# Two block-triangular inverses with products on crossed quadrants, predicated copies for the corrections, and later correction products

## Chip, cores and metric

One NeuronCore of a Trainium2 chip runs the whole kernel in one launch. The metric is the device time of an execution in microseconds, the median of several.

## What is computed

Six layers on 256 tokens of width 1024, float32 in and out: layers 0 and 3 are gated DeltaNet layers ("gdn"), layer 1 is HGRN2, layer 2 is GLA, layers 4 and 5 mix four heads' kinds. Each has a projection, a mixer, an output projection and a SwiGLU feed-forward. The change touches the gdn mixer. Its core, cut from the reference:

```python
L = jnp.where(strict, jnp.einsum('bhncd,bhnsd->bhncs', kb, k) * decay, 0.0)
rhs = jnp.concatenate([v * beta[..., None], kb * jnp.exp(G)[..., None]], axis=-1)
sol = lax.linalg.triangular_solve(L + jnp.eye(CHUNK), rhs, left_side=True, lower=True)
```

The kernel works with chunks of 128 tokens, so it needs (I + L)^-1 for 16 matrices of 128x128: 8 heads times 2 chunks, numbered j.

## The kernel before

**The inverse.** A 128x128 inverse is made of its two diagonal 64x64 blocks, which sit on partitions 0 to 63 and 64 to 127, and one off-diagonal block. The 64x64 blocks grow by doubling: at level lv, blocks of size 2^lv are joined to blocks of twice the size. X is the inverse so far, XT its transpose, and C the part of L that this level joins; the correction is X C X. The 16 matrices go in four groups of four (`GROUPS = (0, 2, 1, 3)`), one PSUM bank a group. For levels 1 to 5 a group takes these steps:

- POOL multiplies `lb` (the 64x64 blocks of L) by the mask of the level into `lb_masked` (L1571), once a level and group.
- PE: the product `cx` of `lb_masked` with X, 8 matmuls of 64x64x64 (L981). A float32 matmul is two records in a profile, each with a weight load.
- ACT copies the product from PSUM to `cx` (tile yb).
- PE: the two corrections, for X and XT, 16 matmuls into the two halves of one bank (`gdn_correct`, L1055).
- DVE subtracts the bank from X and XT in one operation of 128x512 (`corrected`).

PE's order is product of group n, then correction of group n-1. Level 6 makes the off-diagonal block with four plus four single matmuls a group (L984, L1050). Then come the products with the values (L994 on). All matmuls of levels 1 to 5 use the array's two diagonal quadrants: rows 0 to 63 to columns 0 to 63, and rows 64 to 127 to columns 64 to 127.

**What sets the order.** Each engine's program is written out by hand, and semaphores tie them: a `tick` with a key raises one, `wait_ge(*sig.at(key))` waits for it. The eight PSUM banks are claimed by PE in turn (`psum.claim`): a claim of a bank waits until the reader of its last use has released it. In a gdn layer the last projection units have other work between them on PE: `gdn_values` (transposes of v), `gdn_columns` (four small transposes, bank "tok") and two `gdn_spread`. DVE runs beside it `setup` (layer 0), `decay_rows`, `unit_qk` (eight multiplications, each behind an ACT pair), `gdn_columns` (copies the bank "tok") and `gdn_values`. Then the loop over eight heads makes scores, `lt` and `at`, and the inverse begins.

Of the kernel before, what the change touches and what calls it, by code (L numbers as in the profile page):

```python
# [24 lines left out]
U32 = mybir.dt.uint32  # L25
# [192 lines left out]
def build(nc, A, out, book, layers=len(CHAIN)):  # L218

    book.restart()  # L220
    with ExitStack() as ctx:
# [46 lines left out]
        level = sb("level", [P, 7, P])  # L268
        level64 = sb("level64", [P, 6, HALF2])
        ident64 = sb("ident64", [P, HALF2])  # L270
# [75 lines left out]
        blocks = (slice(0, HALF2), slice(HALF2, HALF))  # L346
        xx = flat(inv[:, 0:16, :]).rearrange("p (g two j n) -> p g two j n", g=4, two=2, j=4)
# [7 lines left out]
        def transposed(j):  # L355
            return xx[:, j // 4, 1, j % 4, :]
# [18 lines left out]
        def halves(ap, lv, which):  # L375


            return ap.rearrange("p h (n two c) -> p h n two c", two=2, c=1 << lv)[:, :, :, which, :]

# [142 lines left out]
        def _(pe):  # L522
# [128 lines left out]
            def project(layer, kind, norm):  # L651
                nonlocal unit
                psum.next = 4
                for n, (c0, w, how, name, idx) in enumerate(units_in(kind)):
# [38 lines left out]
                    if kind == "gdn" and n >= N_CONV + 1:  # L693
                        qk_sums(layer, ((0, 1, 2), (3, 4, 5), (6, 7), ())[n - N_CONV - 1])
                    if kind == "gdn" and n == N_CONV + 3:
# [209 lines left out]

            def normed_rows(n):
# [48 lines left out]
            def gdn(layer):  # L955
# [11 lines left out]
                for lv in range(1, 7):  # L967
                    for n, g in enumerate(GROUPS):
                        if lv == 1 and n == 2:
                            gdn_transpose(layer, g)  # L970
                            gdn_correct(layer, lv, GROUPS[1])
                            gdn_transpose(layer, GROUPS[3])
                        b = psum.claim(pe, "cx", layer, lv, g)
                        if lv < 6:
                            pe.wait_ge(*pool_gdn.at("masked", layer, lv, g))
                        pe.wait_ge(*(act_gdn.at("X", layer, g) if lv == 1 else dve_gdn.at("X", layer, lv - 1, g)))
                        for j in range(4 * g, 4 * g + 4):
                            cols_of = slice((j % 4) * HALF2, (j % 4 + 1) * HALF2)
                            if lv < 6:
                                for r in blocks:  # L980
                                    m = nc.tensor.matmul(b[r, cols_of], lb_masked[r, j, :], inverse(j)[r, :], start=True, stop=True)  # L981
                            else:
                                t0 = (j // 8) * T
                                m = nc.tensor.matmul(b[HALF2:HALF, cols_of], lt[0:HALF2, j % 8, t0 + HALF2:t0 + HALF], inverse(j)[0:HALF2, :],  # L984
                                                     start=True, stop=True)
                        m.then_inc(*pe_gdn.tick("cx", layer, lv, g))
                        if n and (lv, n) != (1, 2):
                            gdn_correct(layer, lv, GROUPS[n - 1])
                    gdn_correct(layer, lv, GROUPS[3])
# [40 lines left out]
            def gdn_transpose(layer, g):  # L1030
# [3 lines left out]
                for j in range(4 * g, 4 * g + 4):  # L1034
                    for r in blocks:
                        m = nc.tensor.matmul(b[r, (j % 4) * HALF2:(j % 4 + 1) * HALF2], transposed(j)[r, :], ident[r, r],
                                             start=True, stop=True)
                m.then_inc(*pe_gdn.tick("transposed", layer, g))

            def gdn_correct(layer, lv, g):  # L1040


                b = psum.claim(pe, "z", layer, lv, g)
                pe.wait_ge(*act_gdn.at("cx", layer, lv, g))
                if lv == 6:
                    pe.wait_ge(*dve_gdn.at("XT", layer, 5, g))
                for j in range(4 * g, 4 * g + 4):
                    c = (j % 4) * HALF2
                    if lv == 6:
                        m = nc.tensor.matmul(b[0:HALF2, c:c + HALF2], cx[HALF2:HALF, j, :], inv[HALF2:HALF, 16 + j, HALF2:HALF],  # L1050
                                             start=True, stop=True)
                        continue
                    for left, right, c in ((transposed(j), cx[:, j, :], c), (cx[:, j, :], transposed(j), c + T)):
                        for r in blocks:
                            m = nc.tensor.matmul(b[r, c:c + HALF2], left[r, :], right[r, :], start=True, stop=True)  # L1055
# [423 lines left out]
        def _(pool):  # L1479
# [45 lines left out]
            for lv in range(7):  # L1525
                h = 1 << lv
                m = level[:, lv, :].rearrange("p (n a c) -> p n a c", a=2, c=h)
# [29 lines left out]
            for layer, (kind, _) in enumerate(CHAIN[:layers]):  # L1557
# [8 lines left out]
                early, late = GROUPS[:2], GROUPS[2:]  # L1566
                steps = [(lv, q) for of in (early, late) for lv in range(2) for q in of]
                for lv, q in steps + [(lv, q) for lv in range(2, 6) for q in GROUPS]:
                    pool.wait_ge(*(act_gdn.at("blocks", layer, q) if lv == 0 else
                                   dve_gdn.at("XT", layer, 0, q) if lv == 1 else pe_gdn.at("cx", layer, lv - 1, q)))  # L1570
                    g.tensor_tensor(lb_masked[:, 4 * q:4 * q + 4, :], lb[:, 4 * q:4 * q + 4, :],  # L1571
                                    level64[:, lv:lv + 1, :].to_broadcast([P, 4, HALF2]), ALU.mult)\
# [1426 lines left out]
```

## Time and profile before

| | |
|---|---|
| median of 3 runs | 2128.95 us (2126.13 to 2129.04) |
| profiled execution | 2127.26 us, its span 2125.6 us |
| PE busy | 2071.8 us, 97% of the span |
| DVE, ACT, POOL busy | 1498.4, 891.4, 177.8 us |
| the chain that ended last | PE 84%, DVE 9%, ACT 3%, issue 2% |

A profile lists when each instruction of each engine ran. "Releaser" is the instruction whose semaphore ended a wait; "issue" is idle time in which the engine waited for nothing that the profile shows. PEclk 1.00 is TensorE at 2.4 GHz, 0.50 at 1.2 GHz.

### The profile page before, as it was taken

Reading aid. Unit: us, or ns where it says so; the run is one execution under the profiler, and the core shown is the slowest. Engines: PE = TensorE matmul, PEld = TensorE weight load, DVE = VectorE, ACT = ScalarE, POOL = GpSimd, SP = SyncE. Lnnn points to the kernel's source line nnn. Section 1 sums busy time; section 2 is a strip of 40 time slices with the busy share of each in tenths; the row PEclk is TensorE's granted clock in tenths of the full one; section 3 lists DMA queues with packets and bytes.
Section 4 is the critical chain, followed back from the end, with each engine's and each line's share of the span. In section 5 each row is a group of like instructions: output and inputs, shape, how many; then the busy total and the mean of one; then the engine's idle time right before and its main releaser. Section 6 shows DMA issues by size and latency. Waiting matters only on the chain.

```text
span 2125.6 us, 35623 instructions
## 1 busy us (share of the span) xinstructions
PE 2071.8 (97%) x14377; PEld 1801.8 (85%) x14377; DVE 1498.4 (70%) x1949; ACT 891.4 (42%) x1174; POOL 177.8 (8%) x152
## 2 busy tenths in 40 slices
PE   8999999999999999999899999998989999999999
PEld 8988888798888798888798978887869998778998
DVE  6968754778745677654697684456688887588887
ACT  3244444334444423444323444445564334664332
POOL 6630000000000000000073300000100000100000
PEclk9999999999999999999999999999999999999999
DMA  8512665552655553655464046654325555414552
GB/s 249 178 42 80 201 195 181 176 185 95 198 181 194 161 179 121 203 192 181 147 188 140 3 161 205 193 181 157 101 77 182 178 190 165 138 50 162 196 178 99
DMA packets 267625, 333.81 MB, mean 157 GB/s; under 512 B 20562, under 2 KB 230613, under 8 KB 267493
## 3 DMA queue, kind: packets, MB, share of 16 engines
q1 hardware_dynamic: 267493, 331.93, 48.2%
q8 instruction: 98, 1.61, 0.3%
q14 instruction: 34, 0.28, 0.0%
HBM read 330.84 MB, written 1.05 MB: 156 GB/s over the span
## 4 chain that ended last, share of the span: by engine, by line
PE 84%; DVE 9%; ACT 3%; issue 2%; SPq 1%; DMA 0%; POOL 0%; DVEq 0%; ACTq 0%
PE bank L586 47%; PE bank L554 26%; DVE pj L2187 2%; PE bank L1055 2%; ACT stat L1578 1%; PE bank L819 1%; PE bank L911 1%; PE bank L981 1%; PE bank L637 1%; PE bank L1136 1%; DVE w_hi L2226 1%; DVE sq L2187 1%; DVE pj L2181 1%; DVE w_lo L2228 1%; DVE xt L2187 1%
## 5 line engine op out<-in xcount | busy, mean ns | idle before, releaser
L2228 DVE TENSOR_TENSOR w_lo<-ring,w_hi 128x2048 fp32r<-128x2048 f32 (+2 forms) x289 | 615.2, 2131 | 373.7 <-ACT w_hi L1623 371.3
L1623 ACT ACTIVATE w_hi<-ring 128x2048 fp32r<-128x2048 f32 (+1 forms) x220 | 418.9, 1905 | 474.8 <-PE bank L586 287.3
L586 PE MATMUL bank<-w_lo,xh 128*128 128x512 f32 x992 | 267.3, 392 | 0.0
L586 PE MATMUL bank<-w_hi,xl 128*128 128x512 f32 x896 | 240.6, 390 | 1.0 <-DVE xl L2177 1.0
L586 PE MATMUL bank<-w_hi,xh 128*128 128x512 f32 x896 | 240.9, 391 | 0.6 <-ACT xh L1578 0.6
L554 PE MATMUL bank<-xh,w_hi 128*128 128x256 f32 x1752 | 240.0, 290 | 1.6 <-DVE pj L2177 0.8
L554 PE MATMUL bank<-xh,w_lo 128*128 128x256 f32 (+2 forms) x1832 | 241.4, 284 | 0.0
L554 PEld LDWEIGHTS bank<-xh,w_hi 128*128 128x128 f32 x1752 | 225.0, 195 | 11.4 <-issue 6.7
L554 PEld LDWEIGHTS bank<-xh,w_lo 128*128 128x128 f32 (+2 forms) x1832 | 228.8, 191 | 0.8
L554 PE MATMUL bank<-xl,w_hi 128*128 128x256 f32 x1752 | 229.3, 283 | 0.0
L554 PEld LDWEIGHTS bank<-xl,w_hi 128*128 128x128 f32 x1752 | 218.5, 192 | 0.4
L586 PEld LDWEIGHTS bank<-w_lo,xh 128*128 128x128 f32 x992 | 184.8, 188 | 38.0 <-DVE w_lo L2228 0.7
L586 PEld LDWEIGHTS bank<-w_hi,xh 128*128 128x128 f32 x896 | 167.1, 188 | 37.5 <-issue 2.0
L586 PEld LDWEIGHTS bank<-w_hi,xl 128*128 128x128 f32 x896 | 167.5, 188 | 36.8 <-DVE xl L2177 2.3
L1545 POOL TENSOR_TENSOR w_lo<-ring,w_hi 128x1536 fp32r<-128x1536 f32 x26 | 104.5, 4017 | 950.3 <-DVE w_hi L2226 950.3
L586 PE MATMUL bank<-w_hi,hid_hi 128*128 128x512 f32 x528 | 167.3, 398 | 2.0 <-DVE hid_lo L2177 2.0
L586 PE MATMUL bank<-w_hi,hid_lo 128*128 128x512 f32 x528 | 163.4, 390 | 0.0
L586 PE MATMUL bank<-w_lo,hid_hi 128*128 128x512 f32 x528 | 163.0, 390 | 0.0
L1578 ACT ACTIVATE yb<-bank 128x256 f32<-128x256 f32 (+4 forms) x146 | 58.9, 403 | 165.2 <-PE bank L586 124.9
L586 PEld LDWEIGHTS bank<-w_hi,hid_lo 128*128 128x128 f32 x528 | 99.1, 188 | 21.5
L586 PEld LDWEIGHTS bank<-w_lo,hid_hi 128*128 128x128 f32 x528 | 99.1, 188 | 21.4
L586 PEld LDWEIGHTS bank<-w_hi,hid_hi 128*128 128x128 f32 x528 | 94.6, 189 | 19.5 <-DVE hid_lo L2177 3.7
(325 smaller groups left out, 2409.2 us busy)
## 6 DMA issues: line engine op xcount, KB each, us to landing
ring<-in_ffn_w_in_dram SPq DMA_DIRECT2D x264, 512.0 KB, 4.4
ring<-in_ffn_w_down_dram SPq DMA_DIRECT2D x88, 512.0 KB, 4.2
ring<-in_gdn_w_in_dram SPq DMA_DIRECT2D x64, 512.0 KB, 5.0
ring<-in_ffn_w_out_dram SPq DMA_DIRECT2D x44, 512.0 KB, 3.9
ring<-in_w_in_dram SPq DMA_DIRECT2D x40, 512.0 KB, 4.8
ring<-in_hgrn_w_in_dram SPq DMA_DIRECT2D x32, 512.0 KB, 4.6
ring<-in_gla_w_in_dram SPq DMA_DIRECT2D x24, 512.0 KB, 4.7
ring<-in_gdn_w_out_dram SPq DMA_DIRECT2D x16, 512.0 KB, 4.5
```

Of the source, the lines that this page charges most:

```text
L554: m = nc.tensor.matmul(cols, *((wk, xk) if tokens == ALL else (xk, wk)), start=(first and step == 0 and k == 0 and (j % 2 == 0)), stop=(la ...
L586: m = nc.tensor.matmul(bank[:, 0:width], xin[:, k0 + k, rows_of], w[:, k, c * width:(c + 1) * width], start=(first and step == 0 and k == ...
L637: m = nc.tensor.transpose(b[:, j * P:(j + 1) * P], src[:, t, c * CHUNK + j * P:c * CHUNK + (j + 1) * P], ident[:, :])
L819: m = nc.tensor.transpose(banks[6][:, j * T + t * HALF:j * T + (t + 1) * HALF], hidt[:, t, j * P:(j + 1) * P], ident[:, :])
L911: nc.tensor.matmul(b[:, 0:T], k[:, 0:HALF], q[:, :], start=True, stop=True)
L981: m = nc.tensor.matmul(b[r, cols_of], lb_masked[r, j, :], inverse(j)[r, :], start=True, stop=True)
L1055: m = nc.tensor.matmul(b[r, c:c + HALF2], left[r, :], right[r, :], start=True, stop=True)
L1545: g.tensor_tensor(w_lo[:, unit % RING, part], ring[:, unit % RING, part], high_part(unit)[:, part], ALU.subtract).then_inc(*pool_lo.tick())
L1578: nc.scalar.activation(out_, in_, func, **kw).then_inc(*sig.tick(*key))
L1623: nc.scalar.activation(taken(high_part(u), u), taken(ring[:, u % RING, :], u), ACT.Copy).then_inc(*act_hi.tick())
L2187: v.scalar_tensor_tensor(out=out_, in0=a, scalar=s1, in1=b, op0=op0, op1=op1).then_inc(*sig.tick(*key))
L2228: v.tensor_tensor(w_lo[:, u % RING, 0:share], w[:, 0:share], high[:, 0:share], ALU.subtract).then_inc(*dve_lo.tick())
```

## The change

- `lb` is now copied with factor -1, so that it holds -L. Levels 1 to 4 use it whole, without a mask; POOL's masks remain for level 5 alone (4 operations in place of 24 a layer), and POOL fills XT with the identity ahead of the stage.
- XT is kept on the other half of the partitions than before, so products and the correction of X go from rows r to the other half's columns (`crossed`), while the correction of XT goes from rows r to columns r. The two corrections go to two banks, "z" and "zt".
- What a whole-block product puts outside the blocks of the level is left out when DVE puts the correction in by `copy_predicated`, under the level's mask for XT and its transpose for X, two operations of 128x128 elements a group, and four of 64x128 in place of two subtractions where the stage starts.
- PE's order is product of group n, then correction of group n-2.
- At level 5 the correction of X for the second half is left out (12 matmuls for 16).
- The transposed masks are made once, in layer 0: four PE transposes behind `qk_sums` of unit N_CONV + 2, and two DVE copies ahead of `gdn_columns` in unit N_CONV + 4. The tile `level` keeps four levels; two more are built in `dec`.

The core of the diff (the first `masks_transposed` is PE's, the second DVE's):

```diff
+            def masks_transposed():
+                b = psum.claim(pe, "level masks")
+                pe.wait_ge(*pool_setup.at("constants"))
+                for lv in range(1, 5):
+                    m = nc.tensor.transpose(b[:, (lv - 1) * P:lv * P], level_mask(lv), ident[:, :])
+                m.then_inc(*pe_setup.tick("level masks"))
...
+                gdn_product(layer, 1, GROUPS[0])
+                gdn_product(layer, 1, GROUPS[1])
+                gdn_correct(layer, 1, GROUPS[0])
+                gdn_transpose(layer, GROUPS[2])
+                gdn_correct(layer, 1, GROUPS[1])
+                gdn_transpose(layer, GROUPS[3])
+                gdn_product(layer, 1, GROUPS[2])
+                gdn_product(layer, 1, GROUPS[3])
+                for lv in range(2, 7):
                     for n, g in enumerate(GROUPS):
...
+                        gdn_product(layer, lv, g)
+                        gdn_correct(layer, lv if n > 1 else lv - 1, GROUPS[n - 2])
+                gdn_correct(layer, 6, GROUPS[2])
+                gdn_correct(layer, 6, GROUPS[3])
...
-                    for left, right, c in ((transposed(j), cx[:, j, :], c), (cx[:, j, :], transposed(j), c + T)):
-                        for r in blocks:
-                            m = nc.tensor.matmul(b[r, c:c + HALF2], left[r, :], right[r, :], start=True, stop=True)
+                    for r, to in crossed:
+                        if lv < 5 or to == blocks[0]:
+                            nc.tensor.matmul(b[to, of], transposed(j)[r, :], cx[r, j, :], start=True, stop=True)
+                        m = nc.tensor.matmul(bt[r, of], cx[r, j, :], transposed(j)[r, :], start=True, stop=True)
...
+            def masks_transposed():
+                dve.wait_ge(*pe_setup.at("level masks"))
+                masks = psum.bank("level masks")[:, :].rearrange("p (l n) -> p l n", l=4)
+                for r in blocks:
+                    v.tensor_copy(level64_t[r, :, :], masks[r, :, r]).then_inc(*dve_setup.tick("level masks"))
+                psum.release(dve_setup, "level masks")
...
+                    if layer == 0 and n == N_CONV + 4:
+                        masks_transposed()
                     if kind == "gdn" and n == N_CONV + 4:
                         gdn_columns(layer)
...
-                        X = xx[:, g, :, :, :].rearrange("p two j n -> p (two j n)")
-                        tt(s, X, X, b[:, :], ALU.subtract, "X", layer, lv, g)
+                        put(("X", lv, g), xx[:, g, 0, :, :], 0, level64_t[:, lv - 1:lv, :], by_head(b))
+                        put(("XT", lv, g), xx[:, g, 1, :, :], 1, level64[:, lv:lv + 1, :], by_head(bt))
```

PE's queue in layer 0, from the sums of squares to the next projection unit. Each row is a kind of matmul with the semaphores that it waits for. Before (L943 are the transposes of v, L933 those of "tok", L951 `gdn_spread`, L554 the projection):

```order
L925 MATMUL bank<-yb,ones 128x512 [waits act_gdn] x2
L943 MATMUL bank<-ident,pj 128x128 [waits act_proj,act_gdn]
L943 MATMUL bank<-ident,pj 128x128 x3
...
L933 MATMUL bank<-ident,rows 128x8 [waits dve_gdn,act_gdn,dve_setup]
L933 MATMUL bank<-ident,rows 128x8 x3
```

Of the change, the same place (L959, L949 and L967 are the same steps):

```order
L941 MATMUL bank<-yb,ones 128x512 [waits act_gdn] x2
L959 MATMUL bank<-ident,pj 128x128 [waits act_proj]
L959 MATMUL bank<-ident,pj 128x128 x3
...
L949 MATMUL bank<-ident,rows 128x8 [waits dve_gdn,dve_setup]
L949 MATMUL bank<-ident,rows 128x8 x3
```

The four mask transposes stand one unit ahead and took a bank more, so the banks have moved on by one. The claim of the bank for "tok" waited for an ACT release (act_gdn); now it waits for the release of the bank "level masks", which is the twelfth tick of dve_setup (the wait for dve_setup that stood there before was for its first tick).

DVE's queue at the same place. Before:

```order
L2638 CAST rows_hi<-rows 8x512 [waits act_gdn,dve_gdn]
L2177 TENSOR_TENSOR rows_lo<-rows,rows_hi 8x512 [waits dve_gdn]
L2177 TENSOR_TENSOR pj<-pj,stat 128x512 [waits act_gdn] x8
L2646 COPY cols<-bank 128x4x8 [waits pe_gdn]
L2177 TENSOR_TENSOR vb<-bank,cols 128x512 [waits pe_gdn,dve_gdn]
```

Of the change:

```order
L2678 CAST rows_hi<-rows 8x512 [waits act_gdn,dve_gdn]
L2207 TENSOR_TENSOR rows_lo<-rows,rows_hi 8x512 [waits dve_gdn]
L2207 TENSOR_TENSOR pj<-pj,stat 128x512 [waits act_gdn] x8
L2286 COPY level_t<-bank 64x256 [waits pe_setup]
L2286 COPY level_t<-bank 64x256
L2686 COPY cols<-bank 128x4x8 [waits pe_gdn]
L2207 TENSOR_TENSOR vb<-bank,cols 128x512 [waits pe_gdn,dve_gdn]
```

The two copies that release the bank stand behind all eight multiplications of `unit_qk`.

PE's queue in the middle of the inverse, product and the first matrix's corrections. Before, and of the change behind it:

```order
L981 MATMUL bank<-inv,ct 64x64 x8
L1055 MATMUL bank<-yb,inv 64x64 x2
L1055 MATMUL bank<-inv,yb 64x64 x2
L1055 MATMUL bank<-yb,inv 64x64 x2
L1055 MATMUL bank<-inv,yb 64x64 x2
```

```order
L1063 MATMUL bank<-inv,ct 64x64 x8
L1083 MATMUL bank<-yb,inv 64x64
L1084 MATMUL bank<-inv,yb 64x64
L1083 MATMUL bank<-yb,inv 64x64
L1084 MATMUL bank<-inv,yb 64x64
```

The count of matmuls of a group and level is the same, 24; the corrections alternate between the two banks and touch all four quadrants within four matmuls.

## Rows read from the trace of the kernel before

**Rows 1.** The page: busy time of engines, and the last chain by engine

```profile
PE 2071.8 (97%) x14377; PEld 1801.8 (85%) x14377; DVE 1498.4 (70%) x1949; ACT 891.4 (42%) x1174; POOL 177.8 (8%) x152
PE 84%; DVE 9%; ACT 3%; issue 2%; SPq 1%; DMA 0%; POOL 0%; DVEq 0%; ACTq 0%
```

**Rows 2.** Windows over both inverses: length, busy and instructions by engine, clock, DMA

```profile
133.73:173.07 39.34, 37.47 (x1097) 35.71 (x1097) 21.62 (x40) 15.96 (x38) 14.96 (x21) 1.00 0.01 4
1176.01:1214.44 38.43, 37.12 (x1098) 35.53 (x1097) 21.61 (x40) 15.96 (x38) 14.95 (x21) 1.00 0.02 4
```

**Rows 3.** Timeline, PE, level 3: start, length, line, operation, count of records

```profile
147.35 0.63 PE L981 MATMUL bank<-inv,ct 64*64 64x64 f32 x16
147.82 0.28 PE L1055 MATMUL bank<-yb,inv 64*64 64x64 f32 x4
...
148.75 0.63 PE L981 MATMUL bank<-inv,ct 64*64 64x64 f32 x16
```

**Rows 4.** Windows, PE alone, between stalls: length, busy (matmul records), clock, DMA

```profile
146.02:149.65 3.63, 3.63 (x125) 1.00 0.02 5
161.43:165.62 4.19, 4.09 (x127) 1.00 0.01 4
165.62:169.51 3.89, 3.83 (x127) 1.00 0.02 4
```

**Rows 5.** DMA of 146 to 170 us: GB/s in 40 slices, and by queue

```profile
GB/s 0 0 27 0 0 0 0 0 27 0 0 0 0 27 0 0 0 0 0 0 0 27 0 0 0 0 0 0 27 0 0 0 0 0 27 0 0 0 0 0
...
q8 instruction: 6, 0.10, 1.5%
```

**Rows 6.** Timeline, PE, at two breaks in the stream (idle before, releaser)

```profile
146.02 0.39 PE L981 MATMUL bank<-inv,ct 64*64 64x64 f32 x7 [0.67 <-issue]
...
1203.50 0.31 PE L1055 MATMUL bank<-yb,inv 64*64 64x64 f32 x4
1203.85 0.33 PE L1055 MATMUL bank<-inv,yb 64*64 64x64 f32 x4
```

**Rows 7.** Timeline, PE, where level 5 meets level 6 (L984: rows 0-63 to columns 64-127)

```profile
169.06 0.22 PE L1055 MATMUL bank<-inv,yb 64*64 64x64 f32 x1
169.11 0.22 PE L984 MATMUL bank<-inv,mats 64*64 64x64 f32 x1
169.11 0.22 PE L1055 MATMUL bank<-inv,yb 64*64 64x64 f32 x2
169.17 0.22 PE L984 MATMUL bank<-inv,mats 64*64 64x64 f32 x1
```

**Rows 8.** Timeline, PE, end of level 6 and the first product behind it

```profile
171.92 1.22 PE L1050 MATMUL bank<-inv,yb 64*64 64x64 f32 x16
173.07 2.05 PE L994 MATMUL bank<-vb,inv 128*128 128x128 f32 x16
```

**Rows 9.** Timelines, PE and DVE, layer 0 ahead of the scores; a pair of 64x256 bank reads

```profile
112.01 0.41 PE L933 MATMUL bank<-ident,rows 8*128 8x8 f32 x4
...
113.55 0.38 PE L554 MATMUL bank<-xh,w_hi 128*128 128x256 f32 x1
...
114.20 0.69 DVE L2177 TENSOR_TENSOR pj<-pj,stat 128x512 f32<-128x512 f32 x1 [0.55 <-ACT stat L1578]
114.81 0.18 DVE L2646 COPY cols<-bank 128x32 f32<-128x32 f32 x1
...
1212.60 0.91 DVE L2181 TENSOR_SCALAR inv<-bank 64x256 f32<-64x256 f32 x2
```

**Rows 10.** Timeline, PE, at a long wait, and the window behind it (clock second from the end)

```profile
1053.70 0.66 PE L637 MATMUL bank<-ident,xt 128*128 128x128 f32 x2 [3.86 <-DVE xt L2187]
1050.20:1057.10 6.90, 3.04 (x13) 2.28 (x13) 6.59 (x12) 3.65 (x6) 0.00 (x0) 0.51 0.26 82
```

**Rows 11.** DVE's predicated copies of 128x256, levels 0 and 1, then 2 and 3 (ns)

```profile
L2838 DVE COPY_PREDICATED mats<-level,bank x8: 739/774/807, 491.4 to 499.4; 128x256 f32<-128x256 uint32 x8
...
L2838 DVE COPY_PREDICATED mats<-level,bank x8: 424/429/441, 501.3 to 508.0; 128x256 f32<-128x256 uint32 x8
```

More of the change, by code:

```diff
@@ L346, in build @@
         blocks = (slice(0, HALF2), slice(HALF2, HALF))
+        crossed = ((blocks[0], blocks[1]), (blocks[1], blocks[0]))
         xx = flat(inv[:, 0:16, :]).rearrange("p (g two j n) -> p g two j n", g=4, two=2, j=4)
@@ L378, in halves, with level_mask @@
             return ap.rearrange("p h (n two c) -> p h n two c", two=2, c=1 << lv)[:, :, :, which, :]
+        def level_mask(lv):
+            return level[:, lv, :] if lv < WHOLE_BLOCKS else dec[:, lv - WHOLE_BLOCKS, 0:P]
         def par(col):
@@ L694, in project @@
                         qk_sums(layer, ((0, 1, 2), (3, 4, 5), (6, 7), ())[n - N_CONV - 1])
+                    if layer == 0 and n == N_CONV + 2:
+                        masks_transposed()
                     if kind == "gdn" and n == N_CONV + 3:
@@ L1034, in gdn_transpose, with gdn_product @@
                 for j in range(4 * g, 4 * g + 4):
-                    for r in blocks:
-                        m = nc.tensor.matmul(b[r, (j % 4) * HALF2:(j % 4 + 1) * HALF2], transposed(j)[r, :], ident[r, r],
+                    for r, to in crossed:
+                        m = nc.tensor.matmul(b[to, (j % 4) * HALF2:(j % 4 + 1) * HALF2], transposed(j)[r, :], ident[r, r],
                                              start=True, stop=True)
                 m.then_inc(*pe_gdn.tick("transposed", layer, g))
+            def gdn_product(layer, lv, g):
+                b = psum.claim(pe, "cx", layer, lv, g)
+                pe.wait_ge(*(act_gdn.at("X", layer, g) if lv == 1 else dve_gdn.at("X", layer, lv - 1, g)))
+                if lv == 1:
+                    pe.wait_ge(*act_gdn.at("blocks", layer, g))
+                if lv == 5:
+                    pe.wait_ge(*pool_gdn.at("masked", layer, g))
+                for j in range(4 * g, 4 * g + 4):
+                    of = slice((j % 4) * HALF2, (j % 4 + 1) * HALF2)
+                    if lv == 6:
+                        t0 = (j // 8) * T
+                        m = nc.tensor.matmul(b[HALF2:HALF, of], lt[0:HALF2, j % 8, t0 + HALF2:t0 + HALF], inverse(j)[0:HALF2, :],
+                                             start=True, stop=True)
+                        continue
+                    for r, to in crossed:
+                        m = nc.tensor.matmul(b[to, of], (lb_masked if lv == 5 else lb)[r, j, :], inverse(j)[r, :], start=True, stop=True)
+                m.then_inc(*pe_gdn.tick("cx", layer, lv, g))
@@ L1524, in _ @@
             keep(rot96[:, 80:96], [[-1, 16]], -64, 1, op=ALU.not_equal, fill_=1.0)
[L1525 removed]
+            for lv in range(6):
                 h = 1 << lv
[L1527 removed]
+                m = level_mask(lv).rearrange("p (n a c) -> p n a c", a=2, c=h)
                 fill(m[:, :, 0, :], 0.0)
@@ L1565, in _ @@
                 g.memset(inv[:, 16:32, 0:HALF2], 0.0).then_inc(*pool_gdn.tick("cleared", layer))
[L1566 to L1570, printed above, removed]
+                for q in GROUPS:
+                    g.tensor_copy(xx[:, q, 1, :, :], ident64[:, :].rearrange("p (a n) -> p a n", a=1).to_broadcast([P, 4, HALF2]))\
+                        .then_inc(*pool_gdn.tick("identity", layer, q))
+                for q in GROUPS:
+                    pool.wait_ge(*act_gdn.at("blocks", layer, q))
                     g.tensor_tensor(lb_masked[:, 4 * q:4 * q + 4, :], lb[:, 4 * q:4 * q + 4, :],
-                                    level64[:, lv:lv + 1, :].to_broadcast([P, 4, HALF2]), ALU.mult)\
-                        .then_inc(*pool_gdn.tick("masked", layer, lv, q))
+                                    level64[:, 5:6, :].to_broadcast([P, 4, HALF2]), ALU.mult)\
+                        .then_inc(*pool_gdn.tick("masked", layer, q))
         @block.scalar
@@ L1961, in diagonal_blocks @@
                     for r in blocks:
-                        run(s, lb[r, 4 * g:4 * g + 4, :], lt[r, h0:h0 + 4, t0 + r.start:t0 + r.stop], ACT.Copy, "blocks", layer, g)
+                        run(s, lb[r, 4 * g:4 * g + 4, :], lt[r, h0:h0 + 4, t0 + r.start:t0 + r.stop], ACT.Copy, "blocks", layer, g,
+                            scale=-1.0)
                 for h in range(8):
```

75 lines of the change are left out of this document (35 added, 40 removed).

## The prediction

> **What bounds the kernel now.** I read the page first: PE is busy for 97% of the span and carries 84% of the chain that ended last [rows 1]. So the change is worth what it takes from, or adds to, PE's own sequence. Then the windows over the two inverses: 39.34 and 38.43 us, PE busy for all but 1.9 and 1.3 us of them, DVE for 21.6, ACT 16.0, POOL 15.0 [rows 2]. Nothing but PE can be the bound there, and the most that is at stake is some 78 us.
>
> What is PE's pace in there? From product to product one group takes 148.75 - 147.35 = 1.40 us for 48 records, of which the 16 of the product take 0.47 [rows 3]: 29.2 ns a record, with two quadrants at work, so about 58 ns a record in one quadrant. Read alone, this says that four quadrants would halve the corrections. Before I believe it I ask what else could set 29 ns.
>
> The stream breaks where nothing is waited for: 0.67 us of "issue" at 146.02, and at 1203.50 four records take 0.35 us where others take 0.12 [rows 6]. Between such breaks lie 125 to 127 matmul records, each with its weight load: 256 instructions, within the few records that a trace misses. It takes 3.63, 4.19 and 3.89 us to go through them [rows 4]. In the same stretch the only DMA traffic is the queue that brings instructions: 6 packets, 0.10 MB, so 16 KB each, which are 256 instructions of 64 bytes, and they come 5 to 8 slices of 0.6 us apart, 3.0 to 4.8 us [rows 5]. So a packet is asked for when a block is begun, and PE stands at a block's end if the next one has not come. At 29.2 ns, 128 records take 3.74 us; a packet's round takes 3.6 to 4.2. The stream of instructions and the array are level now, and from 146.02 to 169.51 six blocks took 3.92 us each. I take the fetch as the bound of the stage.
>
> The Trainium skill speaks against this: "Runtime: NRT & Kernel Launch", section "Instruction fetch mechanics", says that the sequencer streams pages of 256 instructions while it runs the current one, that a boundary's cost is mostly hidden, and gives PE a store of 2048 instructions. The trace has the pages of 256, but not the hiding: the breaks at 146.02 and 1203.50. By that page the stage would go at the array's pace, which is the third rival below.
>
> **The change part by part.**
>
> *Levels 1 to 5.* A group and level keeps 24 matmuls, 96 instructions, and its waits. At a fixed round a block, four levels of quicker array buy nothing: 3.9 us for 256 instructions before and after. I take 3.9, the mean of the three lengths; bounds 3.5, between the near packets of rows 5, and 4.2. The start of the stage (transposes, ACT's blocks of `lb`) keeps its ACT and PE steps; the one packet that ends late (the break at 146.02) is in the same place. Nothing there.
>
> *Fewer instructions.* Level 5 drops 4 matmuls in each of four groups, 64 instructions; the second claim of a bank and the split waits add about 16. That is 48 fewer of some 2,200, and they are missed at the end, after the last block has arrived, where level 6 goes one quadrant at a time: 16 records took 1.22 us [rows 8]. 24 records at 58 ns are 1.4 us. In layer 0 the masks' transposes shift the blocks by 10 instructions and leave 1.1. Sum over both layers: -2.5 us, bounds 0 and -4.
>
> *DVE.* One 128x512 subtraction of 0.69 us makes way for two predicated copies of 128 elements. The trace has them with 256 elements: 0.77 us at levels 0 and 1 and 0.43 at 2 and 3 [rows 11]. Half the elements cannot cost more, so a pair is at most 1.54 and 0.86, and likelier 0.9 and 0.6. A group has 1.4 us of PE time, and DVE is busy for 21.6 of 39 us [rows 2]: hidden. If this cover were gone, a pair that is 0.2 us too slow for its group would cost 0.2 x 4 a level. *POOL* loses 20 masks a layer; PE had no wait for them past the first level. Nothing. *Corrections two groups behind* give ACT's copy a longer time; PE's waits in the stage are under 2 us with the breaks [rows 2], and in a stream held by fetches such a wait was already under the fetch. Nothing.
>
> *The masks' transposes, and the bank that they hold.* This is the dear part, and it is in layer 0 alone. The transposes of 128x128 cost PE 4 x 0.11 us. Their bank is released by two DVE copies that stand behind the eight multiplications of `unit_qk`, and the turn of the banks gives just this bank to "tok". PE does "tok" at 112.01 and the next projection unit at 113.55; DVE ends the eighth multiplication at 114.81 [rows 9]. The copies read 64x256 from a bank; two such reads took 0.91 us [rows 9]. `setup` has two small copies more, 0.1 us. So the release comes at 114.81 + 0.1 + 0.9, and "tok" starts at 115.9, which is 3.9 us late. From there PE needs 1.3 us of work to the projection unit, of which 0.25 was a wait: it starts at 117.2 for 113.55. **+3.6 us**, the transposes' 0.44 hidden in it. Queued behind the wait on PE are "tok", two spreads, the projection unit and then the scores, and PE has no wait afterwards in which this could drown. Bounds: +3.0 if the copies take 0.3 each, +4.0.
>
> *The clock.* In that wait PE stands for about 3.4 us, from 112.5 to 115.9. The trace has a wait of 3.86 us that ends at 1053.7; over 6.9 us around it the granted clock was 0.51, and of these PE had work in about 3.4, which then took twice its time [rows 10]. [...] I take +1.3; bounds 0 and 3.4.
>
> **Sum.** +3.6 + 1.3 - 2.5 = +2.4 us. The profiled execution of 2127.26 us (span 2125.6 and 1.7 around it) would take 2129.7. The median of the runs shown lies 1.7 above the profiled one, so I forecast **2131.3 us**. 0.2% is 4.3 us, about what a measurement of this kernel can tell from no change: no change that can be told.
>
> **The rivals.**
>
> *Quicker rounds (15%).* If a packet is asked for earlier once PE drains a block faster, a round may be 3.5 us, as the nearest packets stand [rows 5]. Seven rounds a layer at 0.4 less: -5.6 us, 2125.7. Against it: the rounds that began behind a break were 3.63 to 4.19 [rows 4].
>
> *The wait is not there (8%).* If "tok" came before or ACT's chain freed DVE earlier, +3.6 and +1.3 fall away: 2126.4. Against it stands the order of the two queues.
>
> *Four quadrants pay (8%).* If the breaks are not what bounds the stream, a quadrant's own pace does. A crossed quadrant then has 16 records of 58 ns a group, 0.93 us for 1.40: -0.47 x 20 groups a layer, and the breaks' 1.0 go too, so -10.4 a layer and 2131.3 - 20.8 + 2.5 = 2113. That quadrants do overlap is shown: around 169.1 L984 in a third quadrant runs beside L1055 in two, 5 records within 0.11 us [rows 7]. This is what the Trainium skill, "TensorEngine Tiling (Array Packing)", section "Key Properties", promises for 64x64 tiles, and here the trace agrees for three. The page "TensorE: Matmul & The Clock Gate" (section "Wait — 56ns, not 53.3ns?") puts a floor of 25 ns between starts; by it the corrections would take 0.80 for 0.93 us a group and the gain would be a quarter of this. The change may also fail to overlap at all, if matmuls start in order; under the fetch that gives the forecast's time too.
>
> *The wait costs the clock for longer (17%).* This one ends slower. If the clock falls for 6.9 us as in rows 10 and all of it meets projection work, the price is 3.4 for 1.3: 2133.4. It decides from 3.2 us on.
>
> **How the numbers follow.** Forecast 52%, within 2127.5 to 2134.5; the rivals 15, 8, 8 and 17%. 8 in 10 reaches to the quick rounds with the full saving at the end below, and to the long clock with rounds of 4.1 above (14 x 0.2 = 2.8): 2122 to 2136. Faster by over 0.2% (under 2124.7): the four quadrants, half of the quick rounds and a little of the rest, 20%. Slower by over 0.2% (over 2133.2): half of the long clock and a sixth to a third of the forecast's case, 25%. Within: 55%.
>
> **What would show it.** In the changed kernel's trace: the windows of both inverses 37 to 38.5 us; breaks every 128 matmul records, now at nearly every block, with idle "issue" in place of busy time and PE's busy share in the stage well down; six to seven instruction packets in 24 us as before; records within a block closer than 29 ns. In layer 0 an idle PE of 3 to 4 us ahead of the "tok" transposes with DVE as its releaser, and perhaps a granted clock of 0.5 behind it; none in layer 3. It is wrong if packets come every 2.5 us, if the stage is under 33 us, or if "tok" does not wait.

## The result and the profile after

| | time | against the kernel before |
|---|---|---|
| the kernel before, in the same runs | 2126.51 us (median of 17) | |
| the changed kernel | 2132.1 us (median of 17, 2129.81 to 2139.32) | 1.0028, interval 1.0021 to 1.0034 |
| its profiled execution | span 2129.3 us | +3.7 over the span of 2125.6 |

The change costs 5.6 us, by the interval 4.5 to 7.2, so it is a change that can be told. The forecast of 2131.3 us lies 0.8 below the median, but part of that closeness is luck: I added +2.4 us to a median of 3 runs, 2128.95, which stands 2.4 above the median of 17. The effect itself is more than twice the 2.4 us that I forecast.

The page of the changed kernel, the lines that answer to [rows 1]:

```profile
PE 2055.0 (97%) x14317; PEld 1784.9 (84%) x14317; DVE 1500.1 (70%) x1995; ACT 890.9 (42%) x1174; POOL 151.3 (7%) x116
...
PE 82%; DVE 11%; issue 3%; ACT 3%; SPq 1%; DMA 0%; DVEq 0%; ACTq 0%
```

PE has 16.8 us less busy time and the kernel is longer: what the array saved became waiting. The windows of both inverses, to be held against [rows 2]:

```profile
137.40:176.49 39.09, 28.95 (x1066) 26.68 (x1065) 21.97 (x62) 15.91 (x38) 1.45 (x2) 1.00 0.01 3
1179.41:1218.88 39.47, 28.58 (x1066) 26.57 (x1065) 21.88 (x62) 15.79 (x38) 1.45 (x2) 1.00 0.02 4
```

PE is busy for 29 of 39 us, where it was for 37.5, and the length has not changed: -0.25 us in layer 0, +1.04 in layer 3. PE's timeline there (start, length, records, idle before and its releaser), one group and then the breaks, from several windows:

```profile
151.45 0.57 PE L1063 MATMUL bank<-inv,ct 64*64 64x64 f32 x13
...
152.38 0.51 PE L1063 MATMUL bank<-inv,ct 64*64 64x64 f32 x11
154.17 0.34 PE L1063 MATMUL bank<-inv,ct 64*64 64x64 f32 x5 [1.27 <-issue]
...
158.11 0.21 PE L1084 MATMUL bank<-inv,yb 64*64 64x64 f32 x1 [1.27 <-issue]
...
162.00 0.27 PE L1084 MATMUL bank<-inv,yb 64*64 64x64 f32 x1 [1.10 <-issue]
```

A group of 48 records takes 152.38 - 151.45 = 0.93 us, where it took 1.40 [rows 3]. Four quadrants do overlap: the 32 records of the corrections take some 0.46 us, 14.5 ns each. Then PE stands for 1.1 to 1.3 us with no releaser. The windows from break to break, as [rows 4] (PE alone; then three of layer 3 with all engines), and the DMA of 150 to 174 us, as [rows 5]:

```profile
150.23:154.17 3.94, 2.67 (x125) 1.00 0.02 4
154.17:158.11 3.94, 2.67 (x124) 1.00 0.02 4
158.11:162.00 3.89, 2.79 (x124) 1.00 0.02 4
...
1193.03:1197.26 4.23, 2.56 (x126) 2.42 (x125) 1.49 (x6) 1.29 (x3) 0.00 (x0) 1.00 0.02 4
1197.26:1201.57 4.31, 2.66 (x124) 2.52 (x124) 1.00 (x4) 2.30 (x5) 0.00 (x0) 1.00 0.02 4
1205.68:1209.34 3.66, 2.69 (x125) 2.59 (x125) 1.59 (x5) 1.15 (x3) 0.00 (x0) 1.00 0.02 4
```

```profile
GB/s 0 0 27 0 0 0 0 0 0 27 0 0 0 0 0 27 0 0 0 0 0 0 27 0 0 0 0 0 27 0 0 0 0 0 0 27 0 0 0 0
...
q8 instruction: 6, 0.10, 1.7%
```

124 to 126 records from one break to the next, 3.9 us in layer 0 and 3.7 to 4.3 in layer 3, six packets of instructions in 24 us, as before. The array needs 2.7 of each 3.9 us.

The other place is layer 0 ahead of the scores, [rows 9] before. PE's timeline, then DVE's:

```profile
104.12 2.18 PE L561 MATMUL bank<-xh,w_hi 128*128 128x256 f32 x16 [0.86 <-ACT stat L1607]
...
111.70 1.91 PE L959 MATMUL bank<-ident,pj 128*128 128x128 f32 x16
115.87 0.38 PE L949 MATMUL bank<-ident,rows 8*128 8x8 f32 x4 [2.26 <-DVE level_t L2286]
...
117.21 2.18 PE L561 MATMUL bank<-xh,w_hi 128*128 128x256 f32 x16
```

```profile
114.90 0.87 DVE L2286 COPY level_t<-bank 64x256 f32<-64x256 f32 x2
```

"tok" starts at 115.87 and the projection unit at 117.21, 3.66 us later than at 113.55, with DVE's mask copies as the releaser. Both profiles are level up to here (99.77 and 99.73 at the last projection records ahead of the sums of squares). From here every step stands 3.4 to 3.7 us later, up to the end of layer 0's inverse (176.49 for 173.07) and the start of layer 3's (1179.41 for 1176.01).

### The profile page after: what moved, and what is told of

It reads as the page before. It is cut to its first block, busy times and chain, and to the rows that moved or that the text cites. A ratio compares the mean times of both kernels' runs of the same rounds, so it can differ in the third digit from the quotient of the medians.

```text
span 2129.3 us, 35554 instructions
## 1 busy us (share of the span) xinstructions
PE 2055.0 (97%) x14317; PEld 1784.9 (84%) x14317; DVE 1500.1 (70%) x1995; ACT 890.9 (42%) x1174; POOL 151.3 (7%) x116
## 4 chain that ended last, share of the span: by engine, by line
PE 82%; DVE 11%; issue 3%; ACT 3%; SPq 1%; DMA 0%; DVEq 0%; ACTq 0%
PE bank L593 47%; PE bank L561 26%; DVE pj L2217 2%; ACT stat L1607 1%; PE bank L828 1%; PE bank L1165 1%; PE bank L644 1%; PE bank L1063 1%; DVE w_hi L2256 1%; DVE sq L2217 1%; DVE pj L2211 1%; PE bank L1084 1%; DVE mats L2207 1%; DVE w_lo L2258 1%; DVE sq L2207 1%
```

## The experiments

Each was timed beside the kernel before on the same chip. The ratio to that kernel is the number to compare; 0.001 is 2.1 us. The medians are of 11 executions, of 9 in e3 and of 5 in e9. The changed kernel and the twelve runs:

| | median us | ratio to before | interval |
|---|---|---|---|
| changed kernel | 2132.10 | 1.0028 | 1.0021 to 1.0034 |
| e1 POOL builds the masks | 2126.52 | 1.0008 | 0.9999 to 1.0017 |
| e2 two quadrants | 2130.39 | 1.0018 | 1.0009 to 1.0027 |
| e3 products as 128x128x64 | 2137.56 | 1.0070 | 1.0044 to 1.0097 |
| e4 copies early | 2126.18 | 1.0003 | 0.9994 to 1.0011 |
| e5 PE kept busy in the wait | 2129.09 | 1.0020 | 1.0011 to 1.0029 |
| e6 two quadrants, copies early | 2125.94 | 1.0002 | 0.9993 to 1.0011 |
| e7 e6, one first copy a group | 2125.08 | 0.9998 | 0.9989 to 1.0007 |
| e8 e6, one group behind | 2129.18 | 1.0018 | 1.0009 to 1.0028 |
| e9 e4 with padding matmuls | 2133.57 | 1.0034 | 1.0021 to 1.0048 |
| e10 before, two groups behind | 2124.84 | 0.9989 | 0.9980 to 0.9998 |
| e11 e7, POOL builds the masks | 2125.16 | 0.9990 | 0.9981 to 0.9999 |
| e12 e10, level 5 halved | 2124.43 | 0.9989 | 0.9980 to 0.9998 |

My theory: the inverse goes by the fetch of instructions, so quadrants bring nothing, and the masks' bank costs the time. The rivals: the stage itself got slower; the array's pace counts; the clock.

### The masks' bank: e1, e4

e1: POOL writes the transposed masks with its own patterns in its idle time of layer 0; PE's transposes, their bank and DVE's copies are gone.

```diff
-                    if layer == 0 and n == N_CONV + 2:
-                        masks_transposed()
...
+                        keep(both[r, :, 0, :], [[-2 * h, n], [0, h]], -h, 1)
+                        keep(both[r, :, 0, :], [[2 * h, n], [0, h]], 2 * h - 1, -1)
```

> The changed kernel, but POOL builds the transposed masks in its idle time of layer 0, so that PE's four mask transposes, their bank and DVE's two copies are gone; the rest is unchanged. Theory A (the masks' bank costs the time): the tok transposes stand near 112.0 again in place of 115.9 and the next projection unit near 113.6 in place of 117.2, the time falls by 3.6 us against the changed kernel (2132.1 to about 2128.5), and what is left over the kernel before is +1 to +2. Rival B (the inverse stage itself is slower, the wait is absorbed somewhere): the unit starts earlier but the time stays within 1 us of 2132.1. Rival C (the clock fell in the wait and costs besides): more than 4.5 us come back.

e4: in DVE's program only.

```diff
+                    if layer == 0 and n == N_CONV + 3:
+                        masks_transposed()
                     if kind == "gdn" and n > N_CONV:
                         unit_qk(...)
-                    if layer == 0 and n == N_CONV + 4:
-                        masks_transposed()
```

> The changed kernel with DVE's two copies of the transposed masks one unit earlier, ahead of the multiplications of unit_qk, so that the bank is free long before tok; PE's transposes and the turn of the banks stay. Theory A: the 2.3 us wait ahead of tok goes, but the bank that the masks took still makes the projection unit at 104.1 wait for ACT (0.86 us) behind 0.5 us of transposes, so that tok starts near 113.5 and 2 us of the 3.6 come back: about 2130. Rival B: all 3.6 come back, 2128.5. Rival C: the copies delay DVE's multiplications and with them the release that follows, and nothing comes back.

Both give back some 5 us (5.6 and 5.9 by medians, 4.3 and 5.3 by ratios), more than the 3.6 and 2 expected. The inverse's four quadrants are in both, so the bank is the cause. PE's timeline of e4 at the place:

```profile
111.75 1.91 PE L959 MATMUL bank<-ident,pj 128*128 128x128 f32 x16
113.59 0.41 PE L949 MATMUL bank<-ident,rows 8*128 8x8 f32 x4
...
114.95 1.22 PE L561 MATMUL bank<-xh,w_hi 128*128 128x256 f32 x8
```

The wait is gone; the unit starts 2.26 us earlier. It is still 1.4 later than before, by the transposes and the 0.86 us wait at 104.12, which I had not seen: the claim moved the turn of the banks, and the unit now waits for an ACT release. In e1 the unit that waited at 104.12 starts at 101.99, and the later one so:

```profile
113.73 2.17 PE L561 MATMUL bank<-xh,w_hi 128*128 128x256 f32 x16 [0.51 <-ACT stat L1613]
```

That is 1.2 us earlier than in e4, yet e1 is no faster; 1.2 us lies within both intervals, so this isn't resolved. Such places can be compared only between profiles that are level ahead of them: in those of e6, e10 and e11 PE is 1.5 us later already at 84 us, with the same program up to there. And 2.26 us of lateness does not explain 5: what else goes with the wait is in e5.

### The clock behind the wait: e5

```diff
                         gdn_values(layer)
+                        if layer == 0:
+                            stay_awake(5, (psum.next + 1) % 8)
```

> The changed kernel with five matmuls of 128x256 (0.4 us each, their result unused) ahead of the tok transposes in layer 0, into the bank of the spread that follows, so that PE has work in the 2.3 us in which it waits for the release of the masks' bank. In two of three profiles of kernels with this wait the granted clock fell to 0.50 right behind it and the projection unit took 3 us longer. Theory A (the wait's price is 3.6 us of lateness and, in many executions, up to 3 us of halved clock): tok still starts near 115.9, the clock stays at 1.00 behind it, and the median falls by 1 to 2.5 us against the changed kernel's 2132.1. Rival B (the clock has no part in the median): no change, or +0.2 from the fillers' own end.

Two of three profiles with the wait of 2.3 us (e2, and e3 with 0.84, 0.50 and 0.52 in the three windows from 115 us) show the clock fall, that of the changed kernel doesn't. First e2, PE's timeline and windows of 3 us (clock third from the end), then the same two views of e5:

```profile
115.90 0.38 PE L949 MATMUL bank<-ident,rows 8*128 8x8 f32 x4 [2.29 <-DVE level_t L2286]
...
118.00 3.78 PE L561 MATMUL bank<-xh,w_hi 128*128 128x256 f32 x16
121.58 2.74 PE L561 MATMUL bank<-xl,w_hi 128*128 128x256 f32 x16
```

```profile
115.00:118.00 3.00, 2.10 (x8) 1.28 (x8) 2.41 (x7) 0.00 (x0) 0.00 (x0) 0.71 0.03 8
118.00:121.00 3.00, 3.00 (x15) 3.00 (x15) 2.77 (x8) 0.00 (x0) 0.00 (x0) 0.50 0.02 5
121.00:124.00 3.00, 3.00 (x19) 3.00 (x19) 0.39 (x2) 0.00 (x0) 0.00 (x0) 0.65 0.00 0
```

```profile
113.29 2.32 PE L654 MATMUL bank<-strict,ones 128*128 128x256 f32 x10
115.72 0.38 PE L951 MATMUL bank<-ident,rows 8*128 8x8 f32 x4
...
117.06 2.18 PE L561 MATMUL bank<-xh,w_hi 128*128 128x256 f32 x16
```

```profile
118.00:121.00 3.00, 3.00 (x28) 3.00 (x26) 2.78 (x8) 0.00 (x0) 0.00 (x0) 1.00 0.00 0
```

In e2 the unit ends with its first sums of squares at 126.08, 3.0 us later than in the changed kernel's profile (123.07), with the same wait. In e5 PE works through the wait, starts "tok" at the same time and keeps 2.4 GHz. It is 1.7 us faster by the ratios, and 2.3 us with each median against that of before in the same runs (2129.09 - 2125.76 = 3.3, for 5.6). The intervals of the two ratios overlap, so this alone doesn't settle it, and one profile with a clock of 1.00 can't either, as the changed kernel's has the same without the filler.

The executions themselves say more. Each has its mean granted clock: of the changed kernel's 17, eight have 0.993 or 0.994 and a median of 2130.8 us, seven have 0.992 and two 0.990, together with a median of 2132.3. In e5 one of 11 is at 0.992 or less, among 101 executions of the kernel before that ran beside the experiments one. Some 7 us at half the clock, as in e2's windows, lower that mean by 0.0016. So the clock costs 3.0 us in e2's profile. What it adds to the median is an estimate: 1.3 us by the executions (2132.1 less 2130.8), 1.7 to 2.3 by e5. Where it fell in the executions without a profile isn't shown, and the two at 0.990, which took 2139 us, 8.4 above the first eight, stay unexplained.

### Two quadrants for four: e2, e6

```diff
-        crossed = ((blocks[0], blocks[1]), (blocks[1], blocks[0]))
+        crossed = ((blocks[0], blocks[0]), (blocks[1], blocks[1]))
```

> The changed kernel with every product and correction of levels 1 to 5 back on the two diagonal quadrants (X and XT on the same partitions); same count of instructions, same order, same copies. Theory A (instruction fetch bounds the stage): the array goes back from about 0.93 to 1.40 us a group of 48 records, and the breaks without a releaser shrink from 1.0 to 1.5 us to almost nothing, but the stage stays at 39 to 40 us and the time within 2 us of the changed kernel's. Rival B (the array's pace counts, four quadrants are what keeps the change from being much slower): 0.47 us x 20 groups x 2 layers = +18.8 us.

> The changed kernel with both edits: all products and corrections of levels 1 to 5 on the two diagonal quadrants, and DVE's copies of the masks one unit earlier. Theory A (in a stage held by instruction fetch four quadrants bring nothing, and a PE that runs dry between blocks pays a little more for each): the same 1 to 2 us below the kernel with early copies alone (2126.2) as the straight one was below the changed kernel, so 2124 to 2125. Rival B (the straight kernel's lead was chance): 2126.2. Rival C (with the wait gone four quadrants pay): slower than 2126.2.

By the array's pace the straight kernel would be 18.8 us slower. It is not slower at all: 1.0018 for 1.0028, and with the copies early 1.0002 for 1.0003. e6's windows of both inverses:

```profile
135.60:173.06 37.46, 36.17 (x1065) 34.85 (x1064) 21.32 (x62) 16.16 (x38) 1.46 (x2) 1.00 0.01 3
1176.32:1214.57 38.25, 36.64 (x1066) 35.02 (x1065) 21.33 (x62) 16.16 (x38) 1.46 (x2) 1.00 0.02 4
```

PE is busy for 36 us instead of 28.5, in the same 38. Four quadrants are worth nothing here that can be measured. e2's lead over the changed kernel did not come again in e6 (rival B of e6); only two of e2's 11 executions have a clock of 0.992, for nine of 17 at 0.992 or less in the changed kernel, which may be all of it.

### More and fewer instructions: e9, e3

e9 puts work into the time in which the array stands idle.

```diff
+                    r, to = crossed[j % 2]
+                    m = nc.tensor.matmul(b[to, T + 8 * (j % 4):T + 8 * (j % 4) + 8], (lb_masked if lv == 5 else lb)[r, j, :],
+                                         inverse(j)[r, 0:8], start=True, stop=True)
```

> The kernel of e4 (four quadrants, copies early) with four small matmuls of 64x64x8 more in each product of levels 1 to 5, into unused columns of the bank: 16 instructions more for 96 a group and level, 320 a layer, on an array that stands idle for 1.0 to 1.5 us of every 3.9. Theory A (a block of 256 instructions takes 3.9 us whatever is in it): 1.25 blocks a layer more, +4.9 us a layer, +9.8 us in all, about 2136. Rival B (the array's pace or the chain over ACT and DVE bounds the stage, the idle time is slack): the 8 small records take some 0.1 us a group in time that is idle anyway, at most +1 us, about 2127.

```profile
135.21:177.93 42.72, 32.95 (x1225) 31.05 (x1224) 21.91 (x62) 16.20 (x38) 1.45 (x2) 1.00 0.02 4
1180.90:1223.33 42.43, 33.44 (x1225) 31.18 (x1224) 21.92 (x62) 16.20 (x38) 1.46 (x2) 1.00 0.02 4
...
150.55:174.84 24.29, 17.69 (x747) 16.91 (x748) 9.83 (x32) 7.67 (x18) 0.00 (x0) 1.00 0.02 4
```

The stages of e4 were 37.25 and 38.08 us: +5.47 and +4.35 for 320 instructions each, 9.8 in sum as theory A has it, while PE still stands for 9 to 10 us of 42. (The same stage took 38.3 us in the mean of four profiles, given below; against that it is +8.5.) The third window is six blocks: 4.05 us each. The times give 6.6 us by ratio, less than the stages; rival B's +1 is out either way. That instructions, not the array, bound this stage is shown. That it is their arrival, and not a fixed cost of each on PE, rests on the shape: records start 14.5 ns apart and then none for some 1 us every 128 records, in the rhythm of the packets.

e3 tried the opposite:

```diff
-                    for r, to in crossed:
-                        m = nc.tensor.matmul(b[to, of], (lb_masked if lv == 5 else lb)[r, j, :], inverse(j)[r, :], start=True, stop=True)
+                    m = nc.tensor.matmul(b[:, of], lb[:, j, :], inverse(j)[:, :], start=True, stop=True)
```

> The changed kernel with the product of levels 1 to 5 made by one matmul of 128x128x64 a matrix in place of two of 64x64x64 (the two blocks stand off the diagonal of a 128x128 stationary matrix whose other blocks are zero, level 5 masked in place by POOL, eight operations of 64x256 in place of four of 128x256). That is 16 instructions fewer of 96 a group and level, 320 of some 2150 a layer, while 8 records of a full array should take as long as 16 of two quadrants. Theory A (fetch, some 3.95 us for 256 instructions): 1.25 rounds a layer less, -4.9 us a layer, -9.8 us in all, to about 2122. Rival B (the array or the chain over ACT and DVE bounds the stage): no change, within 1 us. Rival C (a 128x128 weight load costs more than two of 64x64): slower.

```profile
140.66:182.62 41.96, 39.94 (x905) 36.67 (x904) 21.72 (x62) 16.12 (x38) 5.79 (x8) 1.00 0.01 3
```

```profile
149.12 1.10 PE L1062 MATMUL bank<-inv,ct 128*128 128x64 f32 x8
```

The first row is the window over layer 0's inverse, the second PE's timeline at one product. Rival C: eight such records start over some 0.93 us (1.10 less the last one's own time), where 16 of 64x64x64 take 0.47. PE's busy time fills the stage again (39.94 of 41.96), so fewer instructions bought a slower array. The premise was wrong, and the run says nothing against the fetch.

### The copies at the start of the stage: e7

```diff
-                    for r, to in crossed:
-                        put(("XT", 0, g), xx[to, g, 1, :, :], 1, level64[r, 0:1, :], lb[r, 4 * g:4 * g + 4, :])
+                    put(("XT", 0, g), xx[:, g, 1, :, :], 1, level64[:, 0:1, :], lb[:, 4 * g:4 * g + 4, :])
```

> The kernel of e6 with the first predicated copy of a group (level 0 into XT) as one operation of 128x128 in place of two of 64x128, which the straight placement allows. In the changed kernel the pair took 0.91 us where the subtraction of the kernel before took 0.42, and PE's transposes of the second group waited 0.4 to 0.65 us a layer for it. Theory A (the start of the stage is bound by DVE, and what it loses there is not made up later): 0.5 us a layer comes back, -1 us against e6. Rival B (the next block of instructions sets the pace behind it anyway): within 0.3 us of e6.

0.9 us by medians, as A has it, but inside both intervals. The profiles speak for it: stages of 36.62 and 37.02 us for 37.46 and 38.25, and the same in a second pair, e11's 36.72 and 37.29 for e2's 38.22 and 38.00. In the changed kernel, DVE's first copies and PE's transposes that waited for them:

```profile
139.09 0.91 DVE L2724 COPY_PREDICATED inv<-level,ct 64x128 f32<-64x128 uint32 x2
```

```profile
140.15 0.68 PE L1043 MATMUL bank<-ident,inv 64*64 64x64 f32 x16 [0.39 <-DVE inv L2724]
```

### The order: e8, e10, e12

e8 takes the order of the kernel before (one group behind) into e6, e10 the order of the change (two behind) into the kernel before, with nothing else.

```diff
                 for lv in range(2, 7):
                     for n, g in enumerate(GROUPS):
                         gdn_product(layer, lv, g)
-                        if n:
-                            gdn_correct(layer, lv, GROUPS[n - 1])
-                    gdn_correct(layer, lv, GROUPS[3])
+                        gdn_correct(layer, lv if n > 1 else lv - 1, GROUPS[n - 2])
```

> The kernel of e6 with PE's order of the kernel before from level 2 on: the correction of a group stands one group behind its product in place of two. Theory A (a stream held by fetches hides ACT's copy either way): within 0.5 us of e6. Rival B (with two quadrants and 1.4 us a group ACT's copy of 0.4 us is not covered at the level's end, where the last correction follows its product at once): slower by up to 0.5 us a level, 10 levels, so up to +5 us.

> The kernel before with one thing of the change: PE's order of products and corrections, two groups behind. Masks, quadrants, subtractions and counts stay. From e6 and e8, where the order was worth 3.2 us. Theory A (at each level's end the last correction waits for ACT's copy, which two groups behind hides, in the kernel before too, where PE stood 0.1 to 0.3 us at the ends of levels): 1 to 3 us faster than the kernel before, 2123 to 2125. Rival B (in the kernel before the stage goes by the fetch, as I predicted, and the order is worth nothing): within 0.5 us. Rival C (POOL's masks, which wait for the product of the level before, come later for the first group than its product): slower.

Rival B of e8 and theory A of e10: the order is worth 3.2 us in the one kernel (medians) and 2.3 in the other (ratio). In e8 PE waits for ACT's copy at levels' ends; the windows of e10:

```profile
163.81 0.34 PE L1085 MATMUL bank<-yb,inv 64*64 64x64 f32 x4 [0.62 <-ACT yb L1609]
```

```profile
135.05:172.06 37.01, 35.72 (x1097) 34.55 (x1096) 21.35 (x40) 16.04 (x38) 14.99 (x21) 1.00 0.02 4
1176.04:1213.89 37.85, 36.76 (x1097) 35.34 (x1096) 21.36 (x40) 16.02 (x38) 14.96 (x21) 1.00 0.02 4
```

37.01 and 37.85 for 39.34 and 38.43 [rows 2]: 2.9 us by the order, from one profile each. e12 below, with the same order, has 38.52 and 37.54, which is 1.7 us.

e12 leaves out the correction of X for the second half at level 5, as the change does:

```diff
-                        for r in blocks:
+                        for r in blocks[:1] if lv == 5 and c < T else blocks:
```

> The kernel of e10 (the kernel before with corrections two groups behind) with one more part of the change: at level 5 the correction of X for the second half is left out, which nobody reads (4 matmuls a group, 64 instructions a layer), and DVE's subtraction there is 64x256 in place of 128x256. Theory A (a block of 256 instructions takes 3.7 to 3.9 us): a quarter of a block a layer, -0.9 us a layer, -1.8 us against e10, ratio to the kernel before about 0.998. Rival B (level 5 is bound by DVE's three operations of 0.4 us a group, 4.8 us a level, which stay three): within 0.5 us of e10.

The time is e10's, as rival B has it, but with intervals of some 2 us theory A's 1.8 isn't excluded by it. The profiles speak for B: the stages are no shorter than e10's, and DVE's level 5 takes the same. DVE there in e10, in e12 and in the changed kernel:

```profile
166.02 4.88 DVE L2184 TENSOR_TENSOR inv<-inv,bank 128x256 f32<-128x256 f32 x12
```

```profile
165.77 4.89 DVE L2184 TENSOR_TENSOR inv<-inv,bank 64x256 f32<-64x256 f32 x12
```

```profile
170.10 5.34 DVE L2207 TENSOR_TENSOR inv<-inv,bank 64x256 f32<-64x256 f32 x12 [1.07 <-PE bank L1084]
```

Twelve operations in a row without a gap. In the changed kernel PE waits for them in level 6, 1.08 us in layer 0 and 0.66 in layer 3:

```profile
172.01 0.47 PE L1059 MATMUL bank<-inv,mats 64*64 64x64 f32 x5 [0.40 <-DVE inv L2207]
173.35 0.59 PE L1059 MATMUL bank<-inv,mats 64*64 64x64 f32 x7 [0.39 <-DVE inv L2207]
```

So the end of the stage goes by DVE there; in e12 PE's wait is 0.30 us a layer.

### What beats both: e10, e11

> The kernel of e7 with the transposed masks built by POOL as in e1, so that PE's four transposes and their bank are gone too. Theory A: the 0.86 us wait of the projection unit at 104 and the 0.5 us of transposes go (the unit stood at 104.1 with them and at 102.0 without in e1), so 1 to 2 us below e7's 2125.1, about 2123.5 and below the kernel before. Rival B (as e1 against e4: 2126.5 against 2126.2, nothing): 2125.

e11 stands at 0.9990 of the kernel before. Against e7 that is 1.7 us by the ratios and nothing by the medians (2125.16 and 2125.08), so A and B aren't told apart. It keeps predicated copies and whole blocks. e10 has the same place, 0.9989, with one edit. Both are faster than the changed kernel, and than the kernel before by 0.1%, with intervals that just leave out 1 (up to 0.9998 and 0.9999).

## Why the prediction was right or wrong

- **The fetch bounds the stage: right,** with 3.9 us for 256 instructions in layer 0 where I took 3.9. The Trainium skill, "Runtime: NRT & Kernel Launch", section "Instruction fetch mechanics", has the boundary mostly hidden; the trace doesn't agree: PE stands for 1.0 to 1.7 us at each boundary. e9 shows that the blocks set the pace. What I missed is how much a round varies: up to 4.3 us in layer 3 of the changed kernel's profile and 4.5 in e1's, with means over four or five rounds from 3.68 (e5, layer 3) to 4.06. I named the bound 4.2 and used it only for the range.
- **Four quadrants pay nothing: right** (e2, e6), as is the forecast that they do overlap. The rival of 2113 us had the array's 0.93 us a group exactly, and not the time.
- **48 instructions fewer, -2.5 us: wrong.** The profile has +0.8 us over both stages. The same PE program of the stage ran in four profiles (changed kernel, e1, e4, e5) in 37.1 to 40.3 us, mean 38.3 for 38.9 before, so -1.2 over both layers, and that with the gain of the order in it (below). Left out alone in e12, 64 instructions a layer gave no gain that can be seen. The step that failed is that the time "after the last block has arrived" is PE's to save: in the changed kernel's level 6 PE waits 1.08 and 0.66 us for DVE's twelve operations of level 5. That they are the whole reason is argued and not shown.
- **DVE hidden: right in the middle, wrong at both ends.** A pair of copies took 0.5 to 0.95 us, under a group's time. But the first two copies take 0.91 us for 0.42, and PE's transposes in the start of the stage, where I wrote "nothing there", come 0.64 us later (140.15 for 135.85 + 3.66); e7 gets 0.45 us a layer back by the medians, within the noise, and about 1 us a stage in its profile.
- **Two groups behind, nothing: wrong.** It is the one part that is seen to pay, 2.3 to 3.2 us. My argument was that a stream held by fetches hides ACT's waits. The kernel before wasn't held by them alone: its array needs 3.74 us a block, so a wait at a level's end comes on top. In e8 those waits are rows of 0.2 to 0.6 us. In the kernel before against e10 only 0.8 of the 2.9 us are idle time (1.9 and 1.3 us for 1.3 and 1.1); the other 2.1 are in PE's busy time, records that start into an empty array, which is argued and not shown.
- **The wait for the masks' bank, +3.6 us: right** in size (3.66) and releaser. The release alone sets the start of "tok", so the lateness ahead of it, 1.4 us from the transposes and the moved turn of the banks, is swallowed; only 2.26 us are idle time, not the 3.4 of the prediction, and only these come back in e4.
- **The clock, +1.3 us: right in kind, its size open.** No run shows 1.3 us as the price of a fall; the profiles show 3.0 (e2) and nothing (the changed kernel), and the median 1.3 to 2.3 by the estimate above. The rival that all of it meets projection work, 3.4 us, had nearly the right price for an execution in which it falls.
- **Sum.** 3.66, 1.3 to 2.3 for the clock and -1.2 for the stages are 3.8 to 4.8 us, for 5.6 measured with an interval of 4.5 to 7.2; 0.8 to 1.8 us have no owner, which is within the noise. 3.6 + 1.3 - 2.5 was the forecast. "No change that can be told" is not what came: at 0.28% it lies beyond the 0.2% line, to which I gave 25%, and its interval leaves out 1.

## What to carry over

Where small matmuls make up a stage, count instructions from break to break before counting array time: a faster array only turns busy time into idle time once a block of 256 arrives slower than it is used. A one-time helper that claims a bank from a rotating set costs what its slowest reader is late, moves every later claim, and can drop the clock of the work behind; give such work to an idle engine, or release the bank at once. When a change bundles several parts, try each alone: here one of them was a gain and the rest hid it.

## Not expected of the hardware

- Whether the clock falls behind the same wait of 2.3 us differs from profile to profile: granted 1.00 in the changed kernel's and 0.50 for some 7 us in those of e2 and e3; in e2 that is 3.0 us of difference.
- Two quadrants, at 29 ns a record, were no slower than four at 14.5. With four, a block took 3.68 to 4.06 us in the mean of four or five rounds (changed kernel, e1, e4, e5), less than the array's 3.74 us of two quadrants in one of eight stages only. e6 kept to 1.40 us a group through most of layer 0, so 3.74 a block, but took 1.51 in layer 3, so 4.0. The fastest of the eight, e5's layer 3, five rounds:

```profile
1190.98:1209.39 18.41, 13.58 (x621) 1.00 0.02 4
```

- A record of 128x128x64 costs four times one of 64x64x64 on two quadrants or more (0.93 us for 8 against 0.47 for 16), so a block-diagonal product halves the instructions and doubles the array time.
- The same stage varies by up to 3 us between profiles, 37.1 to 40.3. It lies in the length of the rounds; why these differ is open.
